# Stick-breaking sums and gate sums of a four-layer fp32 kernel: from fp32 products to pairs of reduced products

## The reference

```
# layer 1, stick-breaking attention, per head and query block
z = einsum(q, k) * scale
before = kpos < qpos
log1m = where(before, log_sigmoid(-z), 0)
rc = cumsum(log1m, reverse=True)              # a sum over later keys
rc_excl = concatenate([rc[1:], 0])
w = where(before, exp(log_sigmoid(z) + rc_excl), 0)
o = w @ v

# layers 2 and 3
mod = silu(c) @ mod_w[i] + mod_b[i]           # (1, 6144)
shift, scale, gate = split(mod, 3)
x = x + gate * y
```

## Time and profile before

| what | value |
|---|---|
| median of 3 runs | 2463.76 us (2462.36 to 2463.91) |
| the profiled execution's own time | 2462.44 us |
| its span in the profile | 2460.6 us |
| granted clock of TensorE | 1.00 in all 40 slices to the digit shown (0.999 mean) |
| PE busy | 99% |
| DVE busy | 70% |
| ACT busy | 48% |
| POOL busy | 30% |
| units' products on PE | 9600, mean length 0.39 to 0.40 us, overlapping |

### The profile page before, as it was taken

One profiled execution on the slowest core, in us unless ns is written; L12 is line 12 of the kernel. 1 busy time (PEld: TensorE's weight loads), 2 busy tenths in 40 slices (PEclk: granted clock), 3 DMA queues, 4 the chain that ended last, 5 costly groups with the idle time before them and its releaser, 6 DMA issues.

```text
span 2460.6 us, 30526 instructions
## 1 busy us (share of the span) xinstructions
PE 2431.1 (99%) x11470; PEld 2026.4 (82%) x11470; DVE 1733.8 (70%) x2123; ACT 1181.7 (48%) x1569; POOL 736.5 (30%) x997
## 2 busy tenths in 40 slices
PE   9999999999999999999999999999999999999998
PEld 7888888888888887888888888888888878888787
DVE  5987876677787877666566666666766576666766
ACT  6656664454445445334443434444455444444553
POOL 2313121233441600632253053224315023223330
PEclk9999999999999999999999999999999999999999
DMA  8545446677767786887588687768755667777664
GB/s 263 150 142 160 143 138 199 204 258 249 253 221 242 260 274 188 270 271 242 172 259 261 198 250 241 238 207 263 249 152 181 198 186 231 229 226 226 202 206 145
DMA packets 250372, 531.79 MB, mean 216 GB/s; under 512 B 16376, under 2 KB 18752, under 8 KB 250096
## 3 DMA queue, kind: packets, MB, share of 16 engines
q1 hardware_dynamic: 249024, 526.06, 67.8%
q0 software_dynamic: 896, 3.20, 0.4%
q10 hardware_dynamic: 304, 0.57, 0.1%
HBM read 527.67 MB, written 2.10 MB: 215 GB/s over the span
## 4 chain that ended last, share of the span: by engine, by line
PE 60%; issue 3%; DVE 1%; ACT 1%; POOL 0%; DVEq 0%; POOLq 0%; ACTq 0%
PE proj L1013 18%; PE proj L1015 18%; PE proj L1014 18%; PE att L1056 2%; PE att L1039 2%; PE att L1178 1%; PE att L1208 0%; DVE slot L1803 0%; ACT w_hi L1275 0%; PE proj L981 0%; PE proj L980 0%; PE proj L979 0%; PE att L1167 0%; ACT mixed L1344 0%; POOL row_rstd L1980 0%
## 5 line engine op out<-in xcount | busy, mean ns | idle before, releaser
L1685 DVE TENSOR_TENSOR w_lo<-raw,w_hi 128x1024 fp32r<-128x1024 f32 x804 | 995.1, 1242 | 540.7 <-ACT w_hi L1275 536.3
L1013 PE MATMUL proj<-w_hi,h 128*128 128x512 f32 x3200 | 1272.6, 398 | 6.9 <-DVE h L1811 2.2
L1015 PE MATMUL proj<-w_hi,h 128*128 128x512 f32 x3200 | 1244.9, 389 | 0.0
L1014 PE MATMUL proj<-w_lo,h 128*128 128x512 f32 x3200 | 1242.7, 388 | 0.0
L1275 ACT ACTIVATE w_hi<-raw 128x1024 fp32r<-128x1024 f32 x804 | 847.7, 1057 | 777.0 <-PE proj L1015 746.3
L1994 POOL COPY slot<-stage 32x256 f32<-32x256 f32 x704 | 525.6, 747 | 864.2 <-DVE stage L1702 825.2
L1013 PEld LDWEIGHTS proj<-w_hi,h 128*128 128x128 f32 x3200 | 601.8, 188 | 127.2 <-DVE w_lo L1685 5.8
L1015 PEld LDWEIGHTS proj<-w_hi,h 128*128 128x128 f32 x3200 | 600.7, 188 | 127.5
L1014 PEld LDWEIGHTS proj<-w_lo,h 128*128 128x128 f32 x3200 | 601.9, 188 | 118.7 <-issue 1.7
L1994 POOL COPY mixed<-stage 32x256 f32<-32x256 f32 x240 | 168.7, 703 | 324.5 <-DVE stage L1888 311.3
L1835 DVE SCALAR_TENSOR_TENSOR mod_acc<-raw,vec,mod_acc 128x1024 f32<-128x1024 f32 x192 | 256.4, 1336 | 0.0
(11 more groups left out here) (225 smaller groups left out, 1264.1 us busy)
## 6 DMA issues: line engine op xcount, KB each, us to landing
raw<-in_a_w_in SPq DMA_DIRECT2D x320, 512.0 KB, 4.7
raw<-in_mod_w SPq DMA_DIRECT2D x192, 512.0 KB, 4.3
raw<-in_w_in_odd SPq DMA_DIRECT2D x128, 512.0 KB, 4.5
raw<-in_b_w_in SPq DMA_DIRECT2D x128, 512.0 KB, 4.2
raw<-in_w_in_even SPq DMA_DIRECT2D x100, 512.0 KB, 3.7
raw<-in_w_out_even SPq DMA_DIRECT2D x32, 512.0 KB, 4.1
raw<-in_w_out_odd SPq DMA_DIRECT2D x32, 512.0 KB, 5.4
raw<-in_a_w_out SPq DMA_DIRECT2D x32, 512.0 KB, 4.1
```

Of the source, the lines that this page charges most:

```text
L1013: pe.matmul(o, x_hi[:, xs], hi[:, kk, :], start=start, stop=False)
L1014: pe.matmul(o, x_hi[:, xs], lo[:, kk, :], start=False, stop=False)
L1015: done = pe.matmul(o, x_lo[:, xs], hi[:, kk, :], start=False, stop=stop)
L1685: dve.tensor_tensor(m.w_lo[ring][:, 0:size], m.raw[i][:, 0:size], m.w_hi[ring][:, 0:size].bitcast(F32), ALU.subtract).then_inc(s.lo_dve, 1)
```

## The change

The sums of the stick-breaking heads and of the gate are no longer fp32 products. ACT copies `plus` (384 columns), or a part of mod_acc (512 columns), rounded into the first columns of a w_hi buffer; DVE writes the rest of it into the w_lo buffer of the same place; and ACT copies the ones and the triangle, which fp32r holds exactly, into columns 512 to 767 of the w_hi buffer (for the gate, only the ones). PE then does two fp32r products, with hi and with lo, where it did one in fp32: six for a head, two for a gate part.

The new items are "rc_split" in slot s+2 of a head and "gate_split" two slots before each "mod_gate". Each takes a place in the ring of four weight halves, in the order of the walk, as a unit's split does, and waits until the fourth taker before it is done. A place is thus no longer n % 4 but a number set by the plan (`place`, `place_free`). The gate parts stand three slots apart and the third modulation ends four slots earlier, at b + 86.

```diff
@@ -43,6 +43,8 @@
...
 KV_K = 2 * UNIT_K
+SUMS_AT = CHUNK
+GATE_STEP = 3
 QUAD = 4
@@ -205,6 +207,8 @@
...
     fine: int = 0
+    place: int = 0
+    place_free: object = None
 
@@ -240,7 +246,7 @@
...
 
-ORDER = ["rows", "warm", "squares", "split", "hlo", "mod_start", "mod", "unit", "evac", "turn", "resid", "sum", "gate", "direct", "mod_fold", "mod_cols",
+ORDER = ["rows", "warm", "squares", "split", "rc_split", "gate_split", "hlo", "mod_start", "mod", "unit", "evac", "turn", "resid", "sum", "gate", "direct", "mod_fold", "mod_cols",
          "xn", "hin", "pv", "av", "ho", "ho_copy", "ho_sum", "ho_norm", "ho_scale", "ex", "zp", "wm", "tr", "rc", "hout", "mod_gate", "hg_mm", "hg_cross", "keysT", "queryT", "kT_copy", "qT_copy",
@@ -368,6 +374,7 @@
...
         plan.at(s + 1, "zp", item=it)
+        plan.at(s + 2, "rc_split", item=it)
         plan.at(s + 3, "rc", item=it)
@@ -438,7 +445,8 @@
...
         for part in range(4):
-            plan.at(slot + 1 + part, "mod_gate", third=j, layer=layer, part=part, banks=(3,))
+            it = plan.at(slot + 1 + GATE_STEP * part, "gate_split", third=j, layer=layer, part=part, banks=(3,))
+            plan.at(slot + 3 + GATE_STEP * part, "mod_gate", item=it)
 
@@ -558,7 +566,7 @@
...
     modulation(plan, 1, a + 82, b - 10)
-    modulation(plan, 2, b + 9, b + 90)
+    modulation(plan, 2, b + 9, b + 86)
     modulation(plan, 3, b + 100, b + 190)
@@ -698,6 +706,21 @@
...
 
+    held = [None] * SPLIT_N
+    taken = 0
+    for kind, it in walk:
+        if kind in ("split", "rc_split", "gate_split") and it.part < UNIT_K or kind == "gate_split":
+            who = it.unit if kind == "split" else it
+            who.place = taken % SPLIT_N
+            who.place_free = held[who.place]
+            if kind == "split":
+                held[who.place] = Use(s.unit_done, who.n + 1)
+            elif kind == "rc_split":
+                held[who.place] = Use(s.rc_done, it.n + 1)
+            else:
+                held[who.place] = Use(s.mod_mm, MOD_MM[it.third] - 3 + it.part)
+            taken += 1
+
     ring = [None] * RAW_N
@@ -756,8 +779,8 @@
...
         self.eps = self.fixed[:, C_EPS:C_EPS + 1]
-        self.tri = self.masks[:, M_TRI:M_TRI + P]
         self.stick_mask = self.masks[:, M_STICK:M_STICK + 3 * P]
+        self.sum_masks = self.masks[:, M_STICK:M_STICK + 4 * P].rearrange("p (b two n) -> p b two n", two=2, n=P)[:, :, 1, :]
 
@@ -912,6 +935,10 @@
...
         self.plus_ready = sem("plus_ready")
+        self.plus_hi = sem("plus_hi")
+        self.plus_lo = sem("plus_lo")
+        self.gate_hi = sem("gate_hi")
+        self.gate_lo = sem("gate_lo")
         self.rc_done = sem("rc_done")
@@ -975,7 +1002,7 @@
...
                 ws = slice(kk * CHUNK, (kk + 1) * CHUNK)
-                w_hi, w_lo = m.w_hi[u.n % SPLIT_N][:, ws], m.w_lo[u.n % SPLIT_N][:, ws]
+                w_hi, w_lo = m.w_hi[u.place][:, ws], m.w_lo[u.place][:, ws]
                 pe.matmul(o, x_hi, w_hi, start=False, stop=False)
@@ -997,7 +1024,7 @@
...
         w.wait_ge(c.psum_sem, c.psum_n)
-    ring = u.n % SPLIT_N
+    ring = u.place
     hi = m.w_hi[ring][:, 0:c.unit_k * c.width].rearrange("p (k n) -> p k n", k=c.unit_k)
@@ -1070,12 +1097,17 @@
...
     elif kind == "rc":
-        w.wait_ge(s.plus_ready, n + 1)
-        w.wait_ge(s.masks_landed, 16)
+        w.wait_ge(s.plus_lo, n + 1)
         rc = m.bank(it.t_banks[0], 0, 3 * P)
-        pe.matmul(rc[:, 2 * P:3 * P], m.tri, plus[:, 2 * P:3 * P], start=True, stop=True)
-        pe.matmul(rc[:, 0:2 * P], m.tri, plus[:, 0:2 * P], start=True, stop=False)
-        pe.matmul(rc[:, P:2 * P], m.ones, plus[:, 2 * P:3 * P], start=False, stop=True).then_inc(s.rc_done, 1)
+        later, first = slice(2 * P, 3 * P), slice(0, 2 * P)
+        hi, lo = m.w_hi[it.place], m.w_lo[it.place]
+        ones, tri = hi[:, SUMS_AT:SUMS_AT + P], hi[:, SUMS_AT + P:SUMS_AT + 2 * P]
+        pe.matmul(rc[:, later], tri, hi[:, later], start=True, stop=False)
+        pe.matmul(rc[:, later], tri, lo[:, later], start=False, stop=True)
+        pe.matmul(rc[:, first], tri, hi[:, first], start=True, stop=False)
+        pe.matmul(rc[:, first], tri, lo[:, first], start=False, stop=False)
+        pe.matmul(rc[:, P:2 * P], ones, hi[:, later], start=False, stop=False)
+        pe.matmul(rc[:, P:2 * P], ones, lo[:, later], start=False, stop=True).then_inc(s.rc_done, 1)
     else:
@@ -1204,8 +1236,11 @@
...
         elif kind == "mod_gate":
-            w.wait_ge(s.mod_done, 2 * KT * (it.third + 1))
-            pe.matmul(m.bank(it.banks[0]), m.ones, m.mod_acc[:, columns(it.part)], start=True, stop=True).then_inc(s.mod_mm, 1)
+            w.wait_ge(s.gate_lo, it.n)
+            hi, lo = m.w_hi[it.place], m.w_lo[it.place]
+            ones = hi[:, SUMS_AT:SUMS_AT + P]
+            pe.matmul(m.bank(it.banks[0]), ones, hi[:, 0:CHUNK], start=True, stop=False)
+            pe.matmul(m.bank(it.banks[0]), ones, lo[:, 0:CHUNK], start=False, stop=True).then_inc(s.mod_mm, 1)
 
@@ -1271,8 +1306,22 @@
...
             w.wait_ge(s.raw_landed[i], 16 * use)
-            w.wait_ge(s.unit_done, u.n - SPLIT_N + 1)
-            act.activation(m.w_hi[u.n % SPLIT_N][:, 0:size], m.raw[i][:, 0:size], ACT.Copy).then_inc(s.hi_ready, 1)
+            if u.place_free is not None:
+                w.wait_ge(u.place_free.sem, u.place_free.count)
+            act.activation(m.w_hi[u.place][:, 0:size], m.raw[i][:, 0:size], ACT.Copy).then_inc(s.hi_ready, 1)
+        elif kind == "rc_split":
+            hi = m.w_hi[it.place]
+            w.wait_ge(it.place_free.sem, it.place_free.count)
+            w.wait_ge(s.masks_landed, 16)
+            act.activation(hi[:, SUMS_AT:SUMS_AT + 2 * P].rearrange("p (b n) -> p b n", b=2), m.sum_masks, ACT.Copy)
+            w.wait_ge(s.plus_ready, it.n + 1)
+            act.activation(hi[:, 0:3 * P], m.stick(it)[1], ACT.Copy).then_inc(s.plus_hi, 1)
+        elif kind == "gate_split":
+            hi = m.w_hi[it.place]
+            w.wait_ge(it.place_free.sem, it.place_free.count)
+            w.wait_ge(s.mod_done, 2 * KT * (it.third + 1))
+            act.activation(hi[:, SUMS_AT:SUMS_AT + P], m.ones, ACT.Copy)
+            act.activation(hi[:, 0:CHUNK], m.mod_acc[:, columns(it.part)], ACT.Copy).then_inc(s.gate_hi, 1)
         elif kind == "evac" and it.chunk.out_n:
@@ -1680,10 +1729,18 @@
...
             size = u.chunk.unit_k * u.chunk.width
-            ring = u.n % SPLIT_N
+            ring = u.place
             w.wait_ge(s.hi_ready, u.n + 1)
...
                               ALU.subtract).then_inc(s.lo_dve, 1)
+        elif kind == "rc_split":
+            w.wait_ge(s.plus_hi, it.n + 1)
+            dve.tensor_tensor(m.w_lo[it.place][:, 0:3 * P], m.stick(it)[1], m.w_hi[it.place][:, 0:3 * P].bitcast(F32),
+                              ALU.subtract).then_inc(s.plus_lo, 1)
+        elif kind == "gate_split":
+            w.wait_ge(s.gate_hi, it.n)
+            dve.tensor_tensor(m.w_lo[it.place][:, 0:CHUNK], m.mod_acc[:, columns(it.part)],
+                              m.w_hi[it.place][:, 0:CHUNK].bitcast(F32), ALU.subtract).then_inc(s.gate_lo, 1)
         elif kind == "rows":
```

## The result

The kernel after takes 2480.53 us (median of 4 runs, 2477.12 to 2483.0); the kernel before, run beside it, takes 2463.81 us. The ratio is 1.0069, 95% interval [1.0057, 1.008]: slower by 16.7 us. I had predicted 2466.4 us with a range of 2456 to 2474.

The account below looks back on a forecast made before the run. PE, busy 99% of the span, was taken as the bound. Gains of 3.4, 3.3 and 1.2 us against losses of 6.4, 3.5, 0.3 and 0.3 gave +2.6 us, so 2466.4 us, range 2456 to 2474.

Parts of the forecast that it names:

- the keys' slack: POOL's keys for the next group: evacuation behind split(s+6) uses 2.3 of 2.6 us; 0.1 us in each of three groups.
- the third layer's gate: Gates: ACT blocked up to one unit, but exponentials wanted a unit later; 0.3 us lost.
- the clock behind a wait: No term given: PE's new waits were counted as lost one for one, anywhere in the kernel.
- The price of the products: Heads' sums on PE: six reduced products in 0.684 us instead of 0.896; gain 3.4 us over 16 heads.
- the waits at the third heads: PE stalls at sums of each group's third head: 0.45, 1.5, 1.6 and 2.8 us, sum 6.4 us.
- my replay: One third head, timed from its z: plus ready at +9.26, sums at +11.1 against +9.56 due; PE stalls 1.5 us.
- The last head: Layer 1's last head: 1.31 us slack between plus and the sums, so PE stalls 0.8 us.
- The other heads: Sums of eleven other heads: stalls 0 to 0.3 us each, but one of 0.6; 1.3 us in all.
- the values product: Last head: gate chunk's evacuation behind split(s+6), so wm and with it av come some 1.4 us late.
- freeing one slot in the fourth layer: Gate product there moves two slots later, where nothing holds its PSUM bank; 1.2 us gained.
- My term of about 10.5 for all waits: New PE stalls in the whole kernel: 6.4 at third heads, 3.5 at other heads, 0.3 for keys, 0.3 for gates.
- Rival 3: Late w_lo returns raw buffers late, so fetches land late; stalls half again as large, +5.3 us, 2471.7 us; chance 0.14.

Follow-up runs that it names:

- hold_only: Against the kernel before: each head takes and holds a ring place but nothing is written there, sums and gates stay fp32; 2471.91 us against 2463.64.
- spare_late: Against the kernel before: fifteen heads' reduced sums with halves in a free activations' place, sums, mask and v products one slot later than spare placement needs; 2468.51 us.
- sums_only: Against the kernel before: the heads' sums as in the changed kernel, gates and third modulation as before; 2479.56 us against 2463.64.

## Why the prediction was wrong

Three terms of the sum failed: the keys' slack (0.3 us for 4.8), the third layer's gate (0.3 for 3.2), and the clock behind a wait, which the sum had at nothing without a reason (some 4.7 us). The price of the products and the waits at the third heads were sound.

**Price of the sums: near, a little low.** Predicted 0.684 us a head, measured 0.68 to 0.76, so 2.4 us gained where I had 3.4. In after the six loads of a head start at 574.30, 574.41, 574.52, 574.63, 574.75 and 574.87, so they keep to the 0.11 us of the earlier trace rows, for products of 128 and of 256 columns alike. The Trainium skill describes a fast weight load in "TensorE: Matmul & The Clock Gate", section "Weight-path perf modes — Fast Weight Load (FWL) and DoubleRow". It doesn't show for fp32r here: these loads are no closer than those of fp32 in the earlier trace rows. (Two differences in my working are 0.003 us too large: the rows give 0.893 and 0.863, not 0.896 and 0.866; it changes nothing.)

**Third heads: right in mechanism, a little small.** Waits predicted 0.45, 1.5, 1.6 and 2.8 us; measured 0.34 (558.40), 1.91 (636.64), 1.68 (717.55) and 3.19 (798.89): 7.1 against 6.4. (The terms of my replay as written add up to +11.23, a wait of 1.67 us, not the +11.1 and 1.5 that I gave.) The last head waited 0.49, predicted 0.8. The other heads, for which I had 1.3, hardly waited, but the values product did, 0.73 twice (predicted 1.4 once).

**Keys for the next group: the step that failed first.** I had the three at 0.1 each, 2.3 us of 2.6 us of slack used. They waited 1.57, 1.65 and 1.56. The second group's keys, timeline of ACT, DVE, POOL (the earlier trace rows before):

```profile
574.46 1.06 ACT L1311 ACTIVATE w_hi<-raw 128x1024 fp32r<-128x1024 f32 x1 [1.31 <-PE proj L1042]
575.42 1.25 ACT L1341 ACTIVATE slot<-proj,row_rstd 128x512 f32<-128x512 f32 x2
576.71 1.25 DVE L1759 STREAM_TRANSPOSE stage<-slot 128x1024 f32<-128x1024 f32 x1
578.11 15.72 POOL L2051 COPY slot<-stage 32x256 f32<-32x256 f32 x16 [11.29 <-DVE stage L1759]
```

Before, the copies began 573.85 - 572.24 = 1.61 us after the sums of their slot; now 578.11 - 574.33 = 3.78 us after. That is the 2.2 us that I had. But the sixteen copies took 15.72 us instead of 13.73. I took the duration of one row as fixed, and it wasn't: in the trace before, sixteen such copies take 8.96 to 15.49 us, and 11.97 to 15.41 in layer 1. A slack of 0.3 us was no cover. hold_only shows that places alone bring this (keys 5.8 us, its copies 15.70 us at 577.90). What lengthens the copies is said in the last section.

**Gates of the third layer: wrong, 0.3 for 3.2.** I credited the new plan with freeing one slot in the fourth layer (right: no wait at 2352.78 or elsewhere in it, -2.3 us in all against -2.85 worked out) and didn't do the same look for the third, where the earlier trace rows show fp32 gates without a wait. Their new slots do meet an attention output, twice.

**What a wait costs beyond its length: put at nothing.** The prediction took each wait as lost one for one, but the units lose more than PE waits. After the wait of 1.91 us the unit starts over two units slip 2.45 + 1.11 = 3.56 us further, after the one of 1.68 us 1.74 + 1.57 = 3.31. The timeline of PE behind the latter:

```profile
718.54 0.47 PE L1041 MATMUL proj<-w_lo,h 128*128 128x512 f32 x1
718.80 0.63 PE L1042 MATMUL proj<-w_hi,h 128*128 128x512 f32 x1
719.23 0.63 PE L1040 MATMUL proj<-w_hi,h 128*128 128x512 f32 x1
719.66 0.63 PE L1041 MATMUL proj<-w_lo,h 128*128 128x512 f32 x1
```

0.43 us from start to start where it is 0.227: PE runs at 1.2 GHz instead of 2.4, a granted clock of 0.50. The windows of after (length in us, PE busy, granted clock, share and GB/s of DMA):

```profile
714.00:724.00 10.00, 8.32 (x33) 0.83 0.78 249
718.80:721.80 3.00, 3.00 (x9) 0.50 0.81 255
795.00:805.00 10.00, 6.81 (x34) 1.00 0.65 206
1226.00:1236.00 10.00, 8.16 (x34) 0.83 0.43 128
```

So the stretch behind 718 us lost 8 x 0.2 = 1.6 us, and the one behind the gate at 1230.59 about 1.2.

**The sum of layer 1.** Measured: -2.25 (the fifteen heads behind the first row) + 7.6 (sums) + 4.8 (keys, 6.1 less the 1.3 of before) + 1.1 (values, 1.45 less the 0.3 of before) + about 3.5 (clock, after 636 and 718 us) = 14.8 of the 17.8. The other 3.0 are restarts (a keys' wait of 1.57 us moved the next unit by 1.81) and steps up to 0.3 us that I haven't followed. Predicted for layer 1 was +6.8. My term of about 10.5 for all waits of the kernel should have been about 24: the 16.7 us lost, the 2.4 that the sums gave, and the 4.5 that I had for the gates.

**Chances.** Rival 3 (slower, stalls half again as large) came nearest in time. Its late fetches are there on ACT: its waits in front of the split for layer 1's input weights went from 7.4 us (4 times) to 24.7 us (13 times). But PE's waits for a unit's w_lo went only from 1.7 to 1.9 us in the whole kernel, so they don't reach PE by the way that I named; what part they have in the late sums of ACT's queue wasn't tried. Slower had 0.25, and the range ended 6.5 us short. The +2.6 was the difference of 7.9 gained and 10.5 lost; the 10.5 rested on several slacks under half a us, all of which can only go wrong in one direction.

## What to carry to other kernels

A buffer place in a ring that a busy engine paces is not free: holding it moves every later taker, and all that stands behind those takers in in-order queues. Before giving work such a place, look for a buffer outside the ring (here nearly the same work without places costs 0.8 us instead of 16, as long as it isn't moved ahead of its slots). Where two items share a bank, put them into slots in which nothing else uses it, and look through every place that a new spacing touches: in spare_late one wait of 4.8 us ate more than all heads together had gained.

## What the runs showed that I had not expected

- **A short wait can cost its length again.** Behind waits of 1.7 to 1.9 us PE ran at 1.2 GHz for five to eight products, 1 to 1.6 us lost. It isn't the length alone: after the wait of 3.19 us at 798.89 the clock stayed at 1.00 (window 795 to 805 above), as it did after the keys' waits of 1.6 us. Nor is it the place in the program. The trace of sums_only has the same three waits, and there the one of 3.19 us is followed by a stretch and the one of 1.69 us isn't (a row of PE, then the window of PE behind it, granted clock 0.50):

```profile
794.71 0.30 PE L1104 MATMUL att<-w_hi 128*128 128x128 f32 x1 [3.19 <-DVE w_lo L1734]
...
796.00:799.00 3.00, 3.00 (x9) 0.50 0.76 251
```

What decides is open; it differs from execution to execution. So a part of each difference between two traces, some 1.5 us a stretch, need not belong to the edit. The same kind of stretch at about 20 us, 1.3 to 1.7 us lost, is in the profile of after and of several others and not in that of before: it is most of the +1.65 of the table's first line. Most runs of before lie near 2462.0 or 2463.8 us and a few near 2465, which would fit one stretch more or less.
- **POOL's copies are no constant.** Sixteen equal copies took 8.96 to 15.49 us before and up to 15.9 us after. No run tried what lengthens them, but the trace of before shows with what it goes: 381 of the 944 copies had no DVE instruction with two tensor inputs (TENSOR_TENSOR, SCALAR_TENSOR_TENSOR) beside them and took 0.39 us in the mean; 413 shared over 0.3 us with one and took 1.18 us in the mean, 1.28 us at the median. The 13.73 us of before have seven copies of over 0.8 us, the 15.72 us of after and the 15.70 us of hold_only nine. So the length of such a row should be forecast from the DVE work that falls beside it.
